# A feature-major token gather and a threshold router in a diffusion block with sixteen experts

## The reference, cut to what matters

```python
def expert_choice_ffn(h, w_router, w_gate, w_up, w_down):
    bsz, n, d = h.shape
    cap = EC_CAPACITY_FACTOR * n // N_EXPERTS          # 2 * 512 // 16 = 64
    aff = jax.nn.softmax((h @ w_router).astype(jnp.float32), axis=-1)
    g, idx = lax.top_k(jnp.swapaxes(aff, 1, 2), cap)   # 64 tokens for each of 16 experts
    xs = jax.vmap(lambda hb, ib: hb[ib])(h, idx)
    a = jnp.einsum('becd,edf->becf', xs, w_gate)
    u = jnp.einsum('becd,edf->becf', xs, w_up)
    y = jnp.einsum('becf,efd->becd', jax.nn.silu(a) * u, w_down) * g[..., None].astype(h.dtype)
    flat = (idx + (jnp.arange(bsz) * n)[:, None, None]).reshape(-1)
    out = jax.ops.segment_sum(y.reshape(-1, d), flat, num_segments=bsz * n)
    return out.reshape(bsz, n, d)
```

## Time and profile before

| | us |
|---|---|
| median of 3 runs | 2512.27 |
| lowest and highest | 2511.79, 2514.25 |
| span of the profiled execution | 2510.8 |
| router: last strip's residual to the first gather | 286.2 to 312.8 |
| expert pairs: first gate matmul to last down matmul | 322.9 to 763 |
| first matmul of FFN1A | 766.1 |

### The profile page before, as it was taken

The page is one execution under the profiler, slowest core; times in us unless marked ns, Lnnn a source line. Parts: engine busy times, 40 slices in busy tenths (PEclk is TensorE's granted clock), DMA queues, the critical chain, the costliest instruction groups (busy, mean ns, idle before and its releaser), DMA issues.

```text
span 2510.8 us, 29196 instructions
## 1 busy us (share of the span) xinstructions
PE 2478.2 (99%) x10958; PEld 1783.1 (71%) x10958; DVE 1155.5 (46%) x1802; ACT 742.0 (30%) x1066; POOL 8.0 (0%) x11
## 2 busy tenths in 40 slices
PE   8999999999999999999999999999999999999999
PEld 4876733333336888888888888888887667888887
DVE  6785612222227544436444434444337665544422
ACT  4245210100114333224333223333224354333311
POOL 0000000000000000000000000000000000000000
PEclk9999999999999999999999999999999999999999
DMA  7530899999993323313232322233322211323332
GB/s 308 176 126 31 320 394 422 421 422 422 422 411 133 100 92 110 104 63 102 92 100 95 115 82 92 93 100 105 104 81 76 80 43 35 98 94 100 105 104 68
DMA packets 84644, 404.12 MB, mean 161 GB/s; under 512 B 9176, under 2 KB 9560, under 8 KB 60896
## 3 DMA queue, kind: packets, MB, share of 16 engines
q1 hardware_dynamic: 84576, 403.22, 43.7%
HBM read 401.08 MB, written 2.10 MB: 161 GB/s over the span
## 4 chain that ended last, share of the span: by engine, by line
PE 92%; DVE 3%; ACT 2%; issue 1%; DMA 1%; SPq 0%; ACTq 0%; DVEq 0%
PE pair L1123 23%; PE pair L1125 23%; PE pair L1124 23%; PE pair L1399 9%; PE pair L1424 4%; PE pair L1350 2%; PE pair L1650 1%; PE pair L1370 1%; PE pair L1788 1%; PE pair L1265 1%; PE pair L1758 1%; PE pair L1759 1%; PE pair L1371 1%; ACT wH L676 0%; DMA stage<-in_gate 0%
## 5 line engine op out<-in xcount | busy, mean ns | idle before, releaser
L1813 DVE TENSOR_TENSOR wL<-stage,wH 128x1024 fp32r<-128x1024 f32 (+3 forms) x301 | 388.9, 1292 | 771.1 <-ACT wH L676 770.7
L1123 PE MATMUL pair<-hH,wH 128*128 128x512 f32 x1672 | 658.4, 394 | 7.8 <-DVE hL L1858 2.4
L1125 PE MATMUL pair<-hH,wL 128*128 128x512 f32 x1672 | 652.0, 390 | 0.0
L1124 PE MATMUL pair<-hL,wH 128*128 128x512 f32 x1672 | 652.0, 390 | 0.0
L676 ACT ACTIVATE wH<-stage 128x1024 fp32r<-128x1024 f32 (+3 forms) x301 | 335.3, 1114 | 846.9 <-PE pair L1125 843.4
L1123 PEld LDWEIGHTS pair<-hH,wH 128*128 128x128 f32 x1672 | 314.6, 188 | 78.4 <-DVE hL L1858 4.1
L1124 PEld LDWEIGHTS pair<-hL,wH 128*128 128x128 f32 x1672 | 314.6, 188 | 67.1 <-issue 2.4
L1125 PEld LDWEIGHTS pair<-hH,wL 128*128 128x128 f32 x1672 | 314.6, 188 | 66.3
L1123 PE MATMUL pair<-gH,wH 128*128 128x512 f32 x704 | 273.9, 389 | 0.0
L1124 PE MATMUL pair<-gL,wH 128*128 128x512 f32 x704 | 273.9, 389 | 0.0
L1125 PE MATMUL pair<-gH,wL 128*128 128x512 f32 x704 | 273.9, 389 | 0.0
(11 more groups left out here) (353 smaller groups left out, 2148.3 us busy)
## 6 DMA issues: line engine op xcount, KB each, us to landing
ring<-in_experts SPq DMA_DIRECT2D x182, 1024.0 KB, 21.0
stage<-in_gate SPq DMA_DIRECT2D x88, 512.0 KB, 3.6
stage<-in_up SPq DMA_DIRECT2D x88, 512.0 KB, 3.6
stage<-in_down SPq DMA_DIRECT2D x64, 704.0 KB, 4.0
adaw<-in_w_ada SPq DMA_DIRECT2D x32, 512.0 KB, 5.4
stage<-in_w_in SPq DMA_DIRECT2D x18, 512.0 KB, 3.9
ring<-in_experts SPq DMA_DIRECT2D x16, 512.0 KB, 11.6
stage<-in_mla_in SPq DMA_DIRECT2D x9, 512.0 KB, 3.6
```

The costliest lines, as they stand in the source:

```text
L1123: pe.matmul(ps, lh, rh, start=first, stop=False)
L1124: pe.matmul(ps, lh, rl, start=False, stop=False)
L1125: return pe.matmul(ps, ll, rh, start=False, stop=last)
L1813: dve.tensor_tensor(low, stage[:, n % STAGE, 0:w], high, ALU.subtract).then_inc(strip_lo, 1)
```

## The change

What it does, in the order of the program:

- **`gate_ada`.** `GATE_AT` becomes [0, 1, 1, 1, 1, 2, 1, 0]; the eighth step runs after the last square.
- **Softmax.** One instruction for all four token blocks in place of four; the exponential is one instruction too, and the sum is taken by DVE.
- **Top 64.** `af` is turned by two transposes into 48 partitions (32 columns for each token block, of which 16 are used), so that experts 0 to 15 stand on partitions 0 to 15 with one half of the tokens and on 32 to 47 with the other. Eight rounds run over 256 columns, the last without a replacement, and read the first half-width input from PSUM. The two sorted lists of 64 are merged: the 64 largest of both are the maxima of one list against the other one reversed, and the smallest of them is the threshold `least`.
- **Numbers.** `least` is turned to tokens (L1355 of the new file); two compares mark the tokens above and at the threshold (`mark`), a short scan sums within a token's row (`total`), and two matmuls with the constants `ones` and `upto` count over tokens (L1358, L1359). `upto` [128, 128] is a new constant of 64 KB. SP loads it (L600) behind tile 18, and it counts on the semaphore `tabs_loaded`, which PE waits for ahead of the two matmuls.
- **SP's order.** Tile 19 goes out behind tile 16 with no wait of its own; behind tile 18 come `upto`, spare tile 15 (which waited for `xs_turned`) and tile 17.
- **`xt`.** It is scaled by the token's reciprocal deviation as ACT copies it, so `pick` is a plain one-hot matrix made by one instruction.
- **Gather.** `xt` is now the weights and `pick` the moving operand, [128, 128] each: 32 matmuls per pair give features by slots, and `xs` and `turn_tokens` are gone.
- **First pair.** Its gather is cut into 8 columns (`gather_first`); two go ahead of gate and up, and column k+2 comes before the tiles of step k.
- **Later pairs.** PE runs gather, turning of the hidden values, down; ACT and DVE copy the hidden values before they write the next pair's `xsT`.

The core of the diff:

```diff
-        GATE_AT = [0, 1, 1, 1, 1, 2, 2, 0]
+        GATE_AT = [0, 1, 1, 1, 1, 2, 1, 0]
...
             spare_tile(0)
             experts(16, 0, slot_of(16))
+            experts(19, 0, slot_of(19))
             sp.wait_ge(norm_summed, NH2 + 1)
             experts(18, 0, slot_of(18))
+            sp.wait_ge(ada_added, 32)
+            sp.dma_start(upto[:, :], A["tabs"][:, NTAB + NBAND:NTAB + NBAND + P]).then_inc(tabs_loaded, 16)
+            spare_tile(1)
             sp.wait_ge(mod_summed, 6)
             experts(17, 0, slot_of(17))
-            sp.wait_ge(pos_turned, 1)
-            experts(19, 0, slot_of(19))
-            sp.wait_ge(xs_turned, 2)
-            spare_tile(1)
...
-            for r in range(8):
-                pe.wait_ge(top_step, 5 + 2 * r)
+            for r in range(3):
+                pe.wait_ge(top_step, 9 + 2 * r)
                 keep_warm(x[:, r, :])
-            pe.wait_ge(top_step, 20)
-            for i in range(NB):
-                mm = pe.transpose(pb[5][:, i * E:(i + 1) * E], pos[:, i * P:(i + 1) * P], tab("ident", E)[0:E, :])
-            mm.then_inc(pos_turned, 1)
+            pe.wait_ge(top_step, 19)
+            pe.transpose(pb[7][:, 0:E], least[:, :], tab("ident", E)[0:E, :]).then_inc(aff_turned, 1)
+            pe.wait_ge(tabs_loaded, 32)
+            pe.wait_ge(marked, 3)
+            pe.matmul(pb[0][:, 0:P], ones[:, :], total[:, :, :].rearrange("p e i -> p (e i)"), start=True, stop=False)
+            pe.matmul(pb[0][:, 0:P], upto[:, :], mark[:, :, :].rearrange("p e i -> p (e i)"), start=False, stop=True).then_inc(counted, 1)
             keep_warm(x[:, 0, :])
-            keep_warm(x[:, 1, :])
             pe.wait_ge(xt_ready, 8)
...
+            def gather_column(k, ps):
+
+                for i in range(NB):
+                    mm = pe.matmul(ps, xt[:, i, k * P:(k + 1) * P], pick[:, i, :], start=(i == 0), stop=(i == NB - 1))
+                return mm
...
-                for half in range(2):
-                    for k in range(NB):
-                        mm = pe.matmul(pb[6 + half][:, :], pick[:, k, :], xt[:, k, half * 512:(half + 1) * 512],
-                                       start=(k == 0), stop=(k == NB - 1))
-                    mm.then_inc(gathered, 1)
-
-            def turn_tokens(it, p):
...
+                for k in range(KD):
+                    mm = gather_column(k, pb[6 + k // 4][:, (k % 4) * P:(k % 4 + 1) * P])
+                    if k % 4 == 3:
+                        mm.then_inc(gathered, 1)
...
+                first = it is None and p == 0
                 for k in range(KD):
-                    if k == 0:
+                    if first:
+                        if k < KD - 2:
+                            gather_first(k + 2)
+                            pe.wait_ge((first_act, first_dve)[k % 2], k // 2 + 1)
+                        else:
+                            pe.wait_ge((xsT_act, xsT_dve)[k % 2], 1)
+                    elif k == 0:
...
             def next_pair(it, p):
                 gather(it, p + 1)
                 turn_hidden(it, p)
-                turn_tokens(it, p + 1)
                 down(it, p)
                 gate_up(it, p + 1)
```

More of the change, by code:

```diff
@@ L15 @@
 from contextlib import ExitStack
+from dataclasses import replace
 import numpy as np
@@ L71, with backwards @@
 NBAND = 8 * SPAN
+def backwards(row):
+    (part, rows), (step, n) = row.ap
+    return replace(row, offset=row.offset + (n - 1) * step, ap=[[part, rows], [-step, n]])
 def window_means():
@@ L201, in build @@
         xt = place("xt", [P, NB, D], F32, G)
-        pos = place("pos", [E, T], F32, HL)
-        scan = place("scan", [E, T], F32, HL + 2 * KB)
-        work = place("work", [E, 2, T], F32, HL + 4 * KB)
-        xs = place("xs", [P, D], F32, G + 16 * KB)
+        work = place("work", [HALVES, 2, T // 2], F32, G + 20 * KB)
+        mark = place("mark", [P, E, 2 * NB], F32, G + 22 * KB)
+        total = place("total", [P, E, 2 * NB], F32, G + 22 * KB + 512)
+        keep = place("keep", [P, E, 2 * NB], F32, G + 23 * KB)
+        upto = place("upto", [P, P], F32, G + 23 * KB + 512)
         xsT = place("xsT", [P, KD, P], F32, HH)
@@ L1302, in turn_x @@
             def turn_x(k):
+                i, half = divmod(k, 2)
                 if k >= 2:
                     pe.wait_ge(xt_ready, k - 1)
-                for i in range(NB):
-                    mm = pe.transpose(pb[4 + 2 * (k % 2)][:, i * P:(i + 1) * P], x[:, k, i * P:(i + 1) * P], tab("ident"))
+                for j in range(4):
+                    mm = pe.transpose(pb[4 + 2 * half][:, j * P:(j + 1) * P], x[:, 4 * half + j, i * P:(i + 1) * P], tab("ident"))
                 mm.then_inc(x_turned, 1)
@@ L1433, in turn_gates @@
                 pe.wait_ge(pickg_ready, count(it, p, 1, 1))
+                if it is not None or p < PAIRS - 1:
+                    pe.wait_ge(xsT_act, count(it, p, 1, 2))
                 for i in range(NB):
@@ L1455, in down_by_columns @@
                         turn_gates(None, p)
-            gather(None, 0)
-            turn_tokens(None, 0)
+            pe.wait_ge(pick_ready, 1)
+            gather_first(0)
+            gather_first(1)
             gate_up(None, 0)
@@ L2102, in _, with per_token @@
             dve.wait_ge(shift_copied, 1)
-            for i in range(NB):
-                dve.scalar_tensor_tensor(out=af[:, i, :], in0=pb[5][:, i * E:(i + 1) * E], scalar=stat[:, 20 + i:21 + i], in1=shift_row[:, :],
-                                         op0=ALU.mult, op1=ALU.add).then_inc(logits_done, 1)
-            dve.wait_ge(logits_done, NB)
-            dve.tensor_reduce(stat[:, 0:4], af[:, :, :], AX_X, ALU.max).then_inc(lmax, 1)
+            dve.wait_ge(logits_done, 1)
+            def per_token(v):
+                return v.unsqueeze(2).broadcast_to([P, NB, E])
@@ L2122, in _ @@
+            dve.wait_ge(top_step, 15)
+            dve.tensor_copy(other[:, :], backwards(top[32:HALVES, :])).then_inc(top_step, 1)
+            dve.wait_ge(top_step, 16)
+            dve.tensor_tensor(other[:, :], other[:, :], top[0:E, :], ALU.max).then_inc(top_step, 1)
             dve.wait_ge(top_step, 17)
-            dve.tensor_scalar(work[:, 1, :], work[:, 0, :], 0.0, None, ALU.is_lt).then_inc(top_step, 1)
+            dve.tensor_reduce(stat[0:E, 29:30], other[:, :], AX_X, ALU.min).then_inc(top_step, 1)
```

170 lines of the change are left out of this document (102 added, 68 removed).

## The result

The changed kernel takes 2525.13 us (median of 4 runs, 2524.09 to 2526.86) against 2512.03 us (4 runs, 2509.56 to 2514.25); the ratio is 1.0049, with an interval of 1.0037 to 1.0061. It is slower, as the likeliest case said, but by 13.1 us in place of 5.1, and outside the range. The profiled execution spans 2524.7 us, 13.9 more than that of before.

A forecast was written before the change was run, and what follows sets the result against it. The DMA stream was taken to end the expert stage, with PE 2.5 us in hand. Stream 4.3 + 0.8 = 5.1 us later, PE 4.2; the later counts: median 2512.27 + 5.1 = 2517.4, range 2513 to 2521.

The forecast's parts named there:

- the likeliest case: The load waits behind the tiles; first gate matmul 3.5 to 5.5 us later, totals 2516 to 2519, chance 0.68.
- The wait: Ahead of the counting matmuls, PE idles about 18 us for upto, which lands at 321.1.
- The clock: After PE's idle time, the clock starts low and comes back on the way; load to first gate matmul takes 6.1 us.
- Later pairs: From one gather to the next, 0.3 us less than 56.1 per pair; seven times, -2.1 us.
- The first rival: upto overtakes the backlog, PE counts near 303, the stream never pauses and gains 3.0 us: 2509.3, chance 0.10.
- its end moves with S: The DMA stream's end follows S, the first gate matmul, 4.3 us later; with 0.8 for slower refill, 5.1.
- a stream that pauses elsewhere: Sign that the forecast is wrong: DMA pauses somewhere other than the forecast idle of some us near 328.
- The section on PE: Second gather 4.3 + 4.5 = 8.8 us later, later pairs -2.1, 2.5 in hand: PE 4.2 us late.
- the gather columns: Five more columns, 40 records, inside the first pair's gate and up add 4.5 us.
- the 2.5 us in hand: At the end of the expert stage, PE idles 2.50 us for the second FFN1A strip, slack against PE's delay.
- PE: 4.2, stream: 5.1, the later counts: At the end of the experts, PE is 4.2 us late and the stream 5.1; the later sets the total.
- the second and the third rival: Load waits in both: clock stays low, 2520.2, chance 0.12; or less delay arrives, clock back at once, 2515.3, chance 0.10.

The follow-up runs named there:

- the early load: The changed kernel with the load of upto issued ahead of the first expert tile, into the router weights' buffer: 2509.61 us, ratio 0.9985.
- `split_gather`: The kernel before with each 512-column gather matmul cut into four of 128, PE's loop kept: 2521.03 us, ratio 1.0029.
- `split_unrolled`: The kernel before with each 512-column gather matmul cut into four of 128 and PE's loop over six pairs written out: 2516.67 us, ratio 1.0008.
- The other three kernels with the early load: Changed kernel, upto ahead of all expert tiles, plus: whole first gather ahead, 2511.41 us; PE's loop written out, 2511.96; gather of the kernel before, 2510.62.
- the old gather: Changed kernel with upto ahead of all expert tiles, but the kernel before's 512-column gather by slots, xs and turned tokens: 2510.62 us, ratio 0.9984.

## Why the prediction was wrong

**Right.** The wait: PE idle for 19.64 us ahead of L1358 with the load as its releaser, in at 320.9 against 321.1 forecast. The landing: 22.6 us, with "above 20" forecast. The clock: 0.51 from 321 to 324 and 1.00 in the next stretch, that is 1.2 and then 2.4 GHz, after 19.64 us without a matmul. The first gate matmul: 326.60 against 327.2, 3.75 us later than before where 4.3 were taken. Later pairs: 55.8 us from one gather to the next, 416.21 to 471.97, 0.3 less than before. The idle DMA near 328. The first rival's mechanism was right as well, though not its condition: with the load in early, the stream never pauses, the first gate matmul stands at 303.85 (307.8 with the ninth tile's 3.9 us, where 307.6 was worked out), and the total falls, by 4.0 us where 3.0 were worked out. The load did not overtake the backlog, so the rule of ring order in the Trainium skill's page "DMA: Bandwidth & Descriptors", section "Queues, rings and completion order", agrees with 22.6 and 22.9 us behind the tiles against 4.7 us ahead of them; the estimate of 2.15 us from its section "Anatomy of one DMA" was met by none of the three. That section's fit is for DMAs issued from GpSimd, while `upto` goes out from SP, and even the early load had two loads of 512 KB ahead of it that had not landed.

**Wrong, the stream: "its end moves with S".** This is the step that failed, and the prediction's own sign of it, "a stream that pauses elsewhere", appeared. The first pause lost 7.1 in place of 3.0 us, 4.1 more, much as forecast; the second lost 7.5 in place of 1.1 us, 6.4 more, and the prediction had none. The stream is full only as far as buffers are free. From S on it has 14 of them, 35 us of work; the next one comes free when down starts. In the kernel before these times met to within about 2 us, so S and first down moved the end alike, and the earlier trace rows could not tell them apart. In the changed kernel S moved by 3.75 and first down by 9.74 us, because five gather columns now stand between them. The section on PE had that number, "8.8 us later", and asked only whether PE itself would be late at the end (4.2 us) and never who else waits for down. With it the sum would have been 8.8 us and the median 2521.1, the upper edge of the range and still 4 us short; the next two paragraphs have the rest.

**A term that was mis-sized: the gather columns.** One column between two steps costs 331.27 - 330.18 = 1.09 us, not 0.9, and each step that it cuts off costs 3.58 in place of 27.6 / 8 = 3.45. Five of one and six of the other are 5.45 + 0.8 = 6.2 us in place of 4.5, and first down is 3.75 + 6.2 - 0.2 = 9.74 us late.

**Missing: what short matmuls cost the stream.** With S and first down accounted for, the strip issue is 13.1 - 9.7 = 3.4 us later. The table puts 2.5 to 4 us of it on every kernel with 128-column gather matmuls whose stream waits for first down, among them `split_gather` and `split_unrolled`, which differ from before in nothing else but the loop. Why they slow the stream was not tried on its own, but the traces narrow it. Between 400 and 740 us the queue for instructions moved 0.26 MB in the changed kernel and 0.10 MB before; spread over the whole stream, 0.16 MB at 421 GB/s are 0.4 us, an estimate. The delay is not spread, though. The landings of the tiles, counted from the ninth tile and set against those of the kernel before, stay mostly level for 20 tiles or more and then step: from 10.8 to 12.1 us at 541.4 and from 12.2 to 13.5 at 731.5 in the changed kernel, and in `split_unrolled` from 1.3 to 2.1 at 473.9, 1.7 to 2.4 at 571.4 and 2.4 to 3.2 at 666.7. Each step stands within 5 us behind a packet of 16 KB of the instruction queue, and such a packet takes 1.0 to 1.1 us; not every packet is followed by a step. By bytes moved the changed kernel's stream is only 11.3 us behind at the last tiles, by landings 13.5, so some parts of a tile arrive later than the others. This fits instruction packets that hold up one part of each tile behind them; it remains an inference.

**Missing: PE at the loop's jump.** 6.8 us were lost there, which I had not considered. Together with 9.9 us at the second gather, some 1.7 us gained in the later pairs (0.25 to 0.3 each), 1.7 us because the first down matmuls of the last pair took 7.07 in place of 5.37 us at a lower clock (PEclk 0.91 from 760 to 780), and the 2.5 us in hand, PE comes out at 9.9 + 6.8 - 1.7 + 1.7 - 2.5 = 14.2, against 13.95 measured. So PE and the stream, 13.1 us late, arrive together in the changed kernel, to within a us, and unrolling the loop, which mends only one of them, gains nothing. The step "PE: 4.2, stream: 5.1, the later counts" had the right form; both numbers were too small, one by the jump and the columns, the other by first down.

**The rest.** The likeliest case, the second and the third rival all rest on the same wrong step, so the range was narrow for a reason that no rival doubted. A rival that asked where the stream runs dry next was missing.

**What is faster.** The early load gives 2509.6 us, some 15 below the changed kernel and by its ratio 0.15% faster than the kernel before (0.05 to 0.25%). The other three kernels with the early load are 1.6 to 4.0 us faster, two of them not clear of noise, so the gain is a few us at most. By the stretches, the pauses of the kernel before cost 1.5 + 1.5 + 1.1 = 4.1 us, and it has none. Counted from the ninth tile its tiles land 3.8 us earlier than before near 450 us, but its strip issue is only 1.3 us earlier: the steps described above take the rest back. With the old gather 2.8 us are left. The router's own saving of several us and the removed transposes stay hidden under the stream.

## What to carry to other kernels

In these runs a stream through a ring of buffers was paced by whoever frees the buffer that comes next, and that was another piece of work than the one that started it: count the free buffers, multiply by the time of one transfer, and see what frees the one after. Look for dips of a saturated resource in stretches of 10 to 20 us; a mean over 400 us hides them. A small constant that a new algorithm needs belongs ahead of the bulk, since behind it, it landed when the bulk did; and once an operand is late, making the work behind it shorter or cutting it up changes little (at most 4 us here), while moving its 64 KB took some 15 us off.

## What the runs showed of the hardware

- A load of 64 KB took 4.7 us ahead of the expert tiles (with two loads of 512 KB before it), 22.6 us behind 18 of them and 22.9 us three tiles earlier in the same queue; its issue kept SP for 2.13 us there, as long as one of a whole tile, and for 0.33 us where the queue was short.
- 32 matmuls of 128 columns just behind the jump back of PE's loop, under a saturated DMA, left PE idle for 6.4 us (4.9 in the changed kernel as the brackets count, 6.8 by the time the gather took); eight of 512 columns at the same place left none, and neither did the 32 in code without the jump.
- The steady state hid a cost: tile landings slipped by 0.7 to 1.3 us at a time, shortly behind packets of 16 KB on the instruction queue, of which the changed kernel has ten between 505 and 700 us and the kernel before none.
- The clock's low stretch near 253 is there in some profiled executions, partly there in others (0.65 to 0.81) and missing in the rest (with one trace per kernel, whether a kernel favours it is not shown), and everything behind it stands later the lower it is: the ninth tile at 281.4 to 282.2 with 1.00, at 283.6 with 0.81, at 284.4 and 284.6 with 0.68 and 0.65, and at 285.1 to 285.5 with 0.50 to 0.56. The early load (first row, PEclk 1.00) and the early load with the loop written out (second row, 0.50) are one of each, and their strip issues, 744.65 and 748.23, differ by that:

```profile
253.00:256.00 3.00, 3.00 (x17) 2.51 (x15) 0.00 (x0) 0.00 (x1) 0.00 (x0) 1.00 0.76 217
...
253.00:256.00 3.00, 3.00 (x9) 2.33 (x8) 1.70 (x2) 0.56 (x1) 0.00 (x0) 0.50 0.32 61
```
